# Two-block transformer on one core: the second block's latent transposes and query products placed inside the recurrence's chain, and its values centred as they are turned

## The reference, cut to what matters

```python
def _wkv7_scan(r, w, k, v, a, b):
    def step(state, inp):
        r_t, w_t, k_t, v_t, a_t, b_t = inp
        sa = jnp.einsum('bhij,bhj->bhi', state, a_t)
        state = (state * w_t[:, :, None, :] + sa[..., None] * b_t[:, :, None, :]
                 + v_t[..., None] * k_t[:, :, None, :])
        y_t = jnp.einsum('bhij,bhj->bhi', state, r_t)
        return state, y_t
...
    mu = jnp.mean(y, axis=-1, keepdims=True)
    var = jnp.mean(jnp.square(y - mu), axis=-1, keepdims=True)
    y = ((y - mu) * lax.rsqrt(var + LNX_EPS)).reshape(B, S, RWKV_DIM).astype(dt) * lnx_w + lnx_b
    bonus = (jnp.sum(r_h * k_h * r_k, axis=-1, keepdims=True) * v_h).reshape(B, S, RWKV_DIM)
    return (y + bonus) * gate
...
    q = (_rmsnorm(q_lat, q_norm) @ w_q_up).reshape(B, S, H, QK_NOPE_DIM + QK_ROPE_DIM)
    kv = (_rmsnorm(kv_lat, kv_norm) @ w_kv_up).reshape(B, S, H, QK_NOPE_DIM + V_HEAD_DIM)
```

## Time and profile before

| | |
|---|---|
| time, median of 3 runs | 2152.63 us (2151.51 to 2153.56) |
| span of the profiled execution | 2150.6 us, first to last instruction |
| what the three runs have around that span | 0.9 to 3.0 us more (launch and end; the page gives the span alone) |
| TensorE busy | 1896.7 us, 88% |
| VectorE busy | 915.6 us, 43% |
| ScalarE busy | 705.2 us, 33% |
| mean granted TensorE clock | 0.961 of full speed |
| second block | from about 1290 us to the end |

### The profile page before, as it was taken

How to read it: one execution, slowest core, us unless ns; L and a number is a source line. 1 busy time by engine, 2 the same in 40 slices (tenths; PEclk the granted TensorE clock), 3 DMA queues, 4 the chain that set the end, 5 groups by cost and what they waited for, 6 DMA issues and landing times.

```text
span 2150.6 us, 37589 instructions
## 1 busy us (share of the span) xinstructions
PE 1896.7 (88%) x16744; PEld 1282.8 (60%) x16744; DVE 915.6 (43%) x1340; ACT 705.2 (33%) x1023; POOL 47.3 (2%) x68
## 2 busy tenths in 40 slices
PE   9999968877768999866766689999999999999998
PEld 7897314332224785312222248677999886779996
DVE  6644201001104754101101137458676574486774
ACT  6644100000003643211111135325544453255443
POOL 2000000000000100000000000000000000000000
PEclk9999989999989999988888899999999999999999
DMA  9266999999999367999999995032853360238540
GB/s 340 98 252 254 420 423 423 425 425 424 428 428 380 120 242 325 427 428 429 428 429 429 429 400 199 4 125 95 265 196 137 123 228 4 92 107 276 185 159 20
DMA packets 142207, 592.53 MB, mean 276 GB/s; under 512 B 5840, under 2 KB 59296, under 8 KB 116720
## 3 DMA queue, kind: packets, MB, share of 16 engines
q1 hardware_dynamic: 140960, 586.68, 68.9%
q0 software_dynamic: 1104, 3.70, 0.5%
HBM read 589.30 MB, written 1.05 MB: 275 GB/s over the span
## 4 chain that ended last, share of the span: by engine, by line
PE 63%; DMA 27%; DVE 4%; ACT 2%; SPq 1%; issue 1%; DVEq 0%; POOL 0%; POOLq 0%; ACTq 0%
PE ps L654 36%; DMA ring<-in_w_up 27%; PE ps L1638 10%; PE ps L3168 3%; PE ps L3217 1%; PE ps L1672 1%; PE ps L1682 1%; PE ps L671 1%; DVE ring_lo L630 1%; PE ps L1567 1%; DMA area<-in_mem 1%; ACT slab_hi L625 1%; PE ps L1211 1%; PE ps L3315 1%; PE ps L3414 0%
## 5 line engine op out<-in xcount | busy, mean ns | idle before, releaser
L1638 PE MATMUL ps<-ring,area 128*32 128x512 f32 x1728 | 275.8, 688 | 154.0 <-DMA ring<-in_w_up 154.0
L630 DVE TENSOR_TENSOR ring_lo<-ring,slab_hi 128x2048 fp32r<-128x2048 f32 (+2 forms) x137 | 302.8, 2213 | 182.4 <-ACT slab_hi L625 182.3
L625 ACT ACTIVATE slab_hi<-ring 128x2048 fp32r<-128x2048 f32 (+2 forms) x137 | 253.3, 1851 | 254.3 <-PE ps L654 237.8
L1638 PEld LDWEIGHTS ps<-ring,area 128*32 128x32 f32 x1728 | 64.8, 124 | 323.5 <-DMA ring<-in_w_up 185.5
L654 PE MATMUL ps<-hT_hi,slab_hi 128*128 128x256 f32 x832 | 234.6, 282 | 0.5 <-DVE ring_lo L630 0.5
L654 PE MATMUL ps<-hT_hi,ring_lo 128*128 128x256 f32 x832 | 233.1, 280 | 0.0
L654 PE MATMUL ps<-hT_lo,slab_hi 128*128 128x256 f32 x832 | 232.9, 280 | 0.0
L2020 ACT ACTIVATE area<-ps 128x512 f32<-128x512 f32 x32 | 19.1, 597 | 548.3 <-PE ps L1638 507.6
L2662 DVE COPY area<-ps 128x256 f32<-128x256 f32 x32 | 13.6, 424 | 411.7 <-PE ps L1543 411.7
L1672 PE MATMUL ps<-ring,area 128*32 128x512 f32 x984 | 122.3, 617 | 55.6 <-DVE area L2693 31.0
L654 PEld LDWEIGHTS ps<-hT_hi,slab_hi 128*128 128x128 f32 x832 | 156.7, 188 | 1.3 <-DVE ring_lo L630 1.1
(11 more groups left out here) (494 smaller groups left out, 3302.7 us busy)
## 6 DMA issues: line engine op xcount, KB each, us to landing
ring<-in_w_down SPq DMA_DIRECT2D x59, 2048.0 KB, 25.5
ring<-in_w_up SPq DMA_DIRECT2D x58, 2048.0 KB, 21.2
ring<-in_w_gate SPq DMA_DIRECT2D x56, 2048.0 KB, 15.7
ring<-in_w_ffn_up SPq DMA_DIRECT2D x44, 1024.0 KB, 8.3
ring<-in_w_in SPq DMA_DIRECT2D x18, 2048.0 KB, 12.8
ring<-in_w_ffn_down SPq DMA_DIRECT2D x10, 2048.0 KB, 8.0
area<-in_w_gate SPq DMA_DIRECT2D x6, 2048.0 KB, 12.9
ring<-in_xattn_w_kv SPq DMA_DIRECT2D x4, 2048.0 KB, 17.1
```

What stands on the lines that cost most here:

```text
L625: return m.nc.scalar.activation(hi, whole, ACT.Copy)
L630: return m.nc.vector.tensor_tensor(lo, whole, hi, ALU.subtract)
L1638: ins = mm(ps[32 * g:32 * g + CAP, 1, :], m.tokT[:, k, :], rows[:, (g % 2) * BANK:(g % 2 + 1) * BANK], start=k == 0, stop=k == KD - 1)
```

## The change

It has two parts, both in each of the second block's two layers.

**Values.** A constant `centre` (identity minus a block of 1/64 for each head, 128 columns) is added to the table of constants. The values' turn is done by 8 products with it (`turn_centred`) in place of 8 transposes. The head sums of `y` (L3389, first use), VectorE's subtraction (L4251) and their signals go; ScalarE's squares wait for `y_cols`.

**Latents and queries.** The 6 transposes of the latents are put behind chunk 1 of the chain, and the first products of the queries behind chunks 3 to 6; three of the eight stay behind the chain. Their release of the three slots goes with the query products. ScalarE takes the query outputs one after the other, and the masks come after the fourth.

```diff
-                        ("lnx_eps", 1)):
+                        ("lnx_eps", 1), ("centre", P)):
...
+    put("centre", np.eye(P) - np.kron(np.eye(P // HD), np.full((HD, HD), 1.0 / HD)))
...
     tensor_rwkv(m, pe, l, landed, used)
-    release.extend((W_GATES + PAIRS - 1, W_GATES, W_GATES + 1))
-    tensor_mla(m, pe, l, used, free_released)
+    tensor_mla(m, pe, l, used)
...
+QUERY_STEPS = {3: ((0, 0),), 4: ((0, 1),), 5: ((1, 0), (1, 1)), 6: ((2, 0),), "rest": ((2, 1), (3, 0), (3, 1))}
+
+def turned_latents(m, pe, l):
+    pe.wait_ge(*m.at("l_norm", l))
+    for b, tiles in ((2, (0, 1)), (3, (2,))):
+        for i, c in enumerate(tiles):
+            for t in range(NT):
+                ins = m.nc.tensor.transpose(m.ps[:, b, i * T + t * P:i * T + (t + 1) * P], m.lat[:, t, c * P:(c + 1) * P], m.ident)
+        ins.then_inc(m.s("l_T"), 1)
+
+def latent_query(m, pe, l, i, k):
+    q_up = lat_slab(m)[2]
+    t, c0, c1 = i // 2, (0, BANK)[i % 2], (BANK, MH * QKD)[i % 2]
+    if k == 0:
+        if i == 0:
+            pe.wait_ge(*m.at("l_cols", l))
+        elif i >= 2:
+            pe.wait_ge(*m.at("q2_rows", l, i - 1))
+    ins = m.nc.tensor.matmul(m.ps[:, 2 + i % 2, 0:c1 - c0], m.latT[:, k, t * P:(t + 1) * P], q_up[:, k, c0:c1], start=k == 0, stop=k == 1)
+    if k == 1:
+        ins.then_inc(m.s("q2_full"), 1)
+    return ins
...
+    def turn_centred(b, src, half):
+        for i in range(2):
+            for t in range(NT):
+                c0 = (NT * i + t) * P
+                ins = mm(ps[:, b, c0:c0 + P], src[:, 2 * half + i, t * P:(t + 1) * P], m.const("centre"), start=True, stop=True)
+        ins.then_inc(s("tok_T"), 1)
...
     for half in range(2):
-        turn(4 + half, m.V, half)
+        turn_centred(4 + half, m.V, half)
...
-    fill("rest")
...
+        if c == 1:
+            turned_latents(m, pe, l)
+        elif c == 2:
+            fill("rest")
+        for i, k in QUERY_STEPS.get(c, ()):
+            ins = latent_query(m, pe, l, i, k)
+            if k == 0:
+                ins.then_inc(used(W_GATES + (1, 0, PAIRS - 1)[i]), 1)
...
-    pe.wait_ge(*at("y_cols", l))
-    head_sums(0, m.y, "gn_full")
...
+    for i, k in QUERY_STEPS["rest"]:
+        latent_query(m, pe, l, i, k)
+    kv_up = lat_slab(m)[1]
+    for i in range(4):
+        t, out = i // 2, ps[:, 2 + i % 2, :]
+        pe.wait_ge(*(at("q2_rows", l, i + 3) if i < 2 else at("kv2_rows", l, 2 * (i - 1))))
+        c0 = (i % 2) * BANK
+        ins = mm(out, m.latT[:, 2, t * P:(t + 1) * P], kv_up[:, 0, c0:c0 + BANK], start=True, stop=True)
+        ins.then_inc(s("kv2_full"), 1)
...
     for i in range(4):
...
-        if i == 2:
-            masks()
...
+    masks()
     for b in range(2):
-        act.wait_ge(*at("y_mid", l, b + 1))
+        act.wait_ge(*at("y_cols", l, b + 1))
...
+    gate_rows("h")
+    for c in range(3):
...
-    for b in range(2):
-        dve.wait_ge(*at("gn_full", l, b + 1))
-        yb = m.y[:, 2 * b:2 * b + 2, :]
-        v.scalar_tensor_tensor(yb, two(ps[:, b, :]), -1.0 / HD, yb, ALU.mult, ALU.add).then_inc(s("y_mid"), 1)
```

More of the change, by code:

```diff
@@ L382 @@
     group(n, second=[(n, c)])
-group("gn_pe", second=[("gn_full", 2), ("bonus_full", 2), ("var_full", 1), ("gn_wide", 2), ("gateup_full", 2)])
+group("gn_pe", second=[("bonus_full", 2), ("var_full", 1), ("gn_wide", 2), ("gateup_full", 2)])
 group("gn_act", second=[("gateup_in", 1), ("mask_set", 4), ("gn_sq", 2), ("gn_root", 1), ("gn_rows", 2), ("y_scaled", PAIRS),
                         ("ya_hi", 2)])
-group("gn_dve", second=[("y_mid", 2), ("bonus_in", 1), ("bonus_read", 1), ("gn_inv", 1), ("y_unit", 1), ("ya_rows", 2),
+group("gn_dve", second=[("bonus_in", 1), ("bonus_read", 1), ("gn_inv", 1), ("y_unit", 1), ("ya_rows", 2),
                         ("ya_cols", 2)])
@@ L3376, in tensor_rwkv, with tensor_mla @@
                 ins.then_inc(s("y_full"), 1)
-    fill("rest")
-def tensor_mla(m, pe, l, used, free_released):
+        if c == 1:
[6 more added lines that the diff above has]
+                ins.then_inc(used(W_GATES + (1, 0, PAIRS - 1)[i]), 1)
+def tensor_mla(m, pe, l, used):
     nc, ps, at, s = m.nc, m.ps, m.at, m.s
@@ L3633, in scalar_second @@
     scalar_rwkv(m, act, l, lambda: split_out(0))
[L3635 to L3639, removed]
     def masks():
@@ L3857, in scalar_rwkv @@
     split_first_out()
+    gate_rows("h")
+    for c in range(3):
+        if c != 1:
+            wait("l_T", c // 2 + 1)
+        gain = m.par2("q_g")[:, c:c + 1] if c < 2 else m.par2("kv_g")
+        go(m.latT[:, c, :], half_bank(m, 2 + c // 2, c % 2), ACT.Copy, scale=gain).then_inc(s("l_cols"), 1)
     gate_rows("rest")
```

## The result

The changed kernel takes 2160.4 us (median of 5 runs, 2155.3 to 2162.7), the kernel before 2152.6 (5 runs, 2150.0 to 2153.6). The ratio is 1.0034, 95% interval 1.0023 to 1.0046: 7.3 us slower (5.0 to 9.9). That is above the forecast of 2156.0, and 1 us above the range's end. A second set, with 21 runs of the kernel before, gave 1.0040 (1.0027 to 1.0053).

The account below looks back on a forecast made before the run. It took TensorE to set the time in the small matrices, with TensorE and VectorE both close to full in the chain. 2 × (0.86 + 0.76) + 0.2 = +3.4 us gave 2156.0 us, range 2153.2 to 2159.4.

Parts of the forecast that it names:

- The values' turn: Values' transposes before the small products: 16 instructions, 1.73 us in place of 0.87, uncovered, +0.86 us a layer.
- layer 1 as a repeat of layer 0: Second block: layer 1 repeats layer 0's rows within some hundredths, so every term counts twice.
- The chain: Chunked state products up to VectorE's copies of `y`: added wide products cost +4.6 us a layer, with 3.7 and 4.9 kept.
- both switching costs: In the chain, leaving the small products costs 0.14 us and getting back 0.10, each time wide products are inserted.
- the way back: In the chain, return from wide to small products: estimated at 0.10 us each time.
- Behind the chain: From the copies of `y` to ScalarE's first key output: 6.10 us in place of 9.94, -3.84 a layer.
- The table: Loading the table of constants, 128 columns wider: +0.2 us, once.
- Slots given back sooner: Ring slots behind the chain: released up to 4 us sooner, loads issued earlier, nothing gained.
- the clock: Before the third key/value product: a 3.0 to 3.1 us pause lowers TensorE's clock, 1.7 us a layer, 2157.7 or 2159.4; chance 0.34.
- The two pauses that were to bracket the danger: Earlier TensorE pauses in the profile before: after 2.24 us the clock stayed at 1.00, after 2.98 us it fell.
- the forecast's own range: Whole kernel, without the rivals: 2154 to 2157.2 us, chance 0.50.
- 2153.2: Whole kernel: lower end of the stated range in us, leaving out the faster case.

Follow-up runs that it names:

- e4_keep: The changed kernel plus three unused products in TensorE's pause before the third key/value product; 2156.1 us, ratio 1.0025 against the kernel before.
- e16_keep_plain: The changed kernel plus three unused products in TensorE's pause, values turned by plain transposes, centring left out; 2152.3 us, ratio 1.0011 against the kernel before.
- e10_turned: The changed kernel with no query products in the chain, only latents' transposes, and ScalarE's key/value outputs before masks and squares; 2154.2 us, ratio 1.0017 against the kernel before.

## Why the prediction was wrong, point by point

- **The values' turn, "+0.86 us a layer ... Both bounds lie there".** Paid in full, as said, and 0.91 by its own records; by the stage 0.8 to 1.1, by the times 2.7 for two layers (2.0 to 3.4) instead of 1.7. The step of 0.11 came from four instructions; 16 in a row take 1.78, not 1.73. The bounds were too narrow. The forecast also took layer 1 as a repeat of layer 0 "within some hundredths"; for the stages behind the turn that is so, but the stretch from the turn to the chain lasts 89.3 and 91.7 us, by its "issue" pauses.
- **The chain, "+4.6 us".** The mechanism was right: wide products stand between chunks, VectorE runs dry. The size is 5.08. The forecast's own working gave 4.9 with both switching costs; it took less, because the way back was an estimate. Steps are now 1.85 us once (forecast 1.84) and 2.10 four times (2.06). Both costs of switching are seen, and the upper end should have been the value. The Trainium skill ("TensorEngine Tiling (Array Packing)", Key Properties) says that changing the tiling mode drains TensorE; the rows agree that a change costs something: 0.81 us for six transposes that take 0.64 by themselves, and 1.05 for 0.86 of query products.
- **Behind the chain, "-3.84".** It was 4.01. Right in place and order: `bonus_in`, masks, squares, key output. Less right is the split into 2.7 us for the removed mean sums and 1.1 for the masks. Alone, each part is worth 0.75, since then the other's wait ends last; only together they give 4.0.
- **The table, "+0.2".** The issue is 0.1 to 0.3 us longer in the profiles; the times (0.9992 to 1.0009) can't tell 0.2 us from nothing.
- **Slots given back sooner.** Nothing seen from it, as said. From layer 0's variance to layer 1's turn are 321.9 us in both profiles, and from layer 1's variance to the end 263.8 and 263.7.
- **The step that failed: the clock.** The pause before the third key/value product was foreseen as a rival (0.34), at 3.0 to 3.1 us; it is 2.70. Its price was forecast as 1.7 us and is 1.70. What failed is the choice between rival and forecast: it put a term of 1.7 to 3.4 us at nothing, because "that one pause was seen, and the work around this one is wider and denser". In its place, the clock fell to 0.50 behind the pause in layer 1 and cost 1.70 us there, and e4_keep and e16_keep_plain, which fill the pause, are 2 to 5 us faster than the same kernels with it. The two pauses that were to bracket the danger were single cases: the one of 2.98 us kept its clock in nine of fourteen profiles, and 1.51 us was followed by a fall in the very profile that was read. With the fixed stages alone the time would have come to about 2156.6, inside the range.
- **Even that rival ended too low.** With two falls it gave 2159.4. Fixed stages 4.0 (not 3.4), 3.4 if the clock falls in both layers, and some 0.9 that the product turns cost beyond their records make +8.3; measured were 7.3 and 8.6. That sum is put together after the fact, and with one fall it would be 6.6, within the intervals as well. The range had its upper end at the rival's central value, and so had no room for the errors of the rival's own terms. Nor do all its other ends have a sum: by the stated terms the forecast's own range ends at 2156.8, not 2157.2, and for 2153.2 no working is given.

What stays open: why the same pause lets the clock fall in one layer and not in another, how often it does so in a timed run, the 0.5 to 1.1 us of the product turn's cost that no stage shows, and the larger part of what e10_turned lost.

## What to carry to other kernels

When an engine's work is moved into a place where it already uses 0.96 of 1.02 us, it costs its full time plus the change of shape on both sides, even if the engines around it had seemed to be what was waited for. Moving work off the far side opens a pause there, and a pause of TensorE has to be priced with its clock: look for it in the plan, and take the fall as a chance and not as a matter of length, since one profile shows only one draw. If other work can't be put there, a few products that nobody needs may cost less than the fall (here six instructions a layer, some 3 us won). And where a rival is nearly as likely as the forecast, the range's end is the rival's end and not its middle.

## What the runs showed of the hardware

- At a pause of 2.70 us TensorE's granted clock fell to 0.50 in two of six layers and stayed at 1.00 in four, in the same place of the program; at 2.98 us it fell in five of fourteen profiles, at 4.33 us in two of two. Behind shorter pauses it fell too: 1.51 us in five of fourteen, and "issue" pauses of 1.70 to 2.18 us in four of five. So the two pauses of the forecast mark no border. The Trainium skill ("TensorE: Matmul & The Clock Gate", Why this matters for your kernels) asks for no long idle gaps between bursts of matmuls, because the clock then goes back to half. The level agrees (0.50), but the gaps that it warns of are longer than 2.70 us, so a kernel planned by it would have been hit here too. The forecast took 2.24 us for a disagreement with that rule; it is none, since that pause is shorter still.
- In the dense stream of small products TensorE has pauses that wait for nothing the profile shows, 0.8 to 4.0 us a layer over all fourteen profiles. They differ from execution to execution of the same instructions (3.3 us in layer 1 of before; 1.9 and 4.0 there in the two profiles of the changed kernel). With the first block's length (the second block's turn began anywhere between 1337.4 and 1342.1 us) they are a part of the spread of 2.1 us between runs.
